# Feature projection in fp32 by Strassen's seven block products, with GpSimd making the weight sums

## What is computed

```python
mod = jax.nn.silu(c) @ p['ada_w'] + p['ada_b']
shift, scale, gate = jnp.split(mod, 3, axis=-1)
h = rms_norm(x, p['norm_w']) * (1 + scale[:, None, :]) + shift[:, None, :]
z = h @ p['w_in']
z_a = centred_conv3(z[..., :A_CONV_COLS], p['conv_a'])
...
y = jnp.concatenate([y_a, y_b, y_c], axis=-1) @ p['w_out']
return x + gate[:, None, :] * y
```

## Time and profile before

| | |
|---|---|
| time, median of 3 runs | 5318.88 us (5315.06 to 5323.39) |
| span of the profiled execution | 5309.2 us |
| TensorE busy | 5077.2 us, 96% |
| VectorE, ScalarE, GpSimd busy | 2811.0, 2089.1, 513.2 us |
| granted TensorE clock, mean | 0.983 |

### The profile page before, as it was taken

The page is one execution under the profiler, slowest core; times in us unless marked ns, Lnnn a source line. Parts: engine busy times, 40 slices in busy tenths (PEclk is TensorE's granted clock), DMA queues, the critical chain, the costliest instruction groups (busy, mean ns, idle before and its releaser), DMA issues. The chain is left out here.

```text
span 5309.2 us, 97761 instructions
## 1 busy us (share of the span) xinstructions
PE 5077.2 (96%) x40460; PEld 2651.3 (50%) x40460; DVE 2811.0 (53%) x4438; ACT 2089.1 (39%) x3590; POOL 513.2 (10%) x950
## 2 busy tenths in 40 slices
PE   8999999989979999989989999999899799999899
PEld 3444444468754444444434444444778544444454
DVE  2222387746645565556522223876566455555565
ACT  1121455346545444421111214553556445445211
POOL 0000000033320000001100000000344100000011
PEclk9999999999989999999999999999999899999999
DMA  6311566466650222145343115664666502221353
GB/s 230 142 68 60 191 207 212 141 172 169 166 138 19 56 57 47 37 142 210 117 164 142 70 60 187 219 200 153 173 168 167 129 14 55 56 50 38 123 174 112
DMA packets 549653, 668.51 MB, mean 126 GB/s; under 512 B 200976, under 2 KB 427792, under 8 KB 539168
## 3 DMA queue, kind: packets, MB, share of 16 engines
q1 hardware_dynamic: 548624, 661.17, 40.0%
q10 hardware_dynamic: 592, 1.10, 0.1%
HBM read 395.01 MB, written 267.13 MB: 125 GB/s over the span
## 5 line engine op out<-in xcount | busy, mean ns | idle before, releaser
L517 PE MATMUL ps<-feat_hT,w_features 128*128 128x512 f32 x2240 | 972.5, 592 | 0.0
L517 PEld LDWEIGHTS ps<-feat_hT,w_features 128*128 128x128 f32 x2240 | 420.4, 190 | 505.9 <-issue 503.2
L1968 DVE TENSOR_REDUCE att_mx<-ps 128x1 f32<-128x1024 f32 x384 | 453.2, 1219 | 282.3 <-PE ps L1844 280.4
L2256 PE MATMUL ps<-w_out,fin_yT 128*128 128x512 f32 x1280 | 568.6, 598 | 1.3 <-ACT fin_yT L2118 1.3
L850 PE MATMUL ps<-w_tokens,prep_hT 128*128 128x512 f32 (+1 forms) x1248 | 534.6, 586 | 0.0
L1863 PEld LDWEIGHTS ps<-kc,att_pr 128*128 128x128 f32 x3264 | 351.5, 141 | 322.8 <-issue 275.8
L1932 ACT ACTIVATE att_PT<-ps 128x512 f32<-128x512 f32 x384 | 229.0, 596 | 632.3 <-PE ps L1863 629.2
L1863 PE MATMUL ps<-kc,att_pr 128*128 128x128 f32 x3264 | 457.2, 280 | 5.8 <-ACT att_PT L1932 2.7
L1923 ACT ACTIVATE att_pr<-ps,att_nb 128x1024 f32<-128x1024 f32 x384 | 424.2, 1109 | 68.3 <-DVE att_nb L1970 68.1
L1977 DVE COPY att_PT<-ps 128x512 f32<-128x512 f32 x384 | 263.9, 687 | 285.1 <-PE ps L1863 284.5
L850 PEld LDWEIGHTS ps<-w_tokens,prep_hT 128*128 128x128 f32 x1248 | 234.8, 190 | 288.9 <-issue 285.2
(11 more groups left out here) (271 smaller groups left out, 6998.2 us busy)
## 6 DMA issues: line engine op xcount, KB each, us to landing
s_sc<-prep_sc SPq DMA_DIRECT2D x20, 3072.0 KB, 9.2
scan_src<-s_sc SPq DMA_DIRECT2D x104, 384.0 KB, 4.9
s_qkt<-scan_qT SPq DMA_DIRECT2D x40, 576.0 KB
s_zf<-feat_co SPq DMA_DIRECT2D x88, 256.0 KB, 2.6
src<-s_sc SPq DMA_DIRECT2D x56, 384.0 KB, 4.9
s_ht<-feat_hT SPq DMA_DIRECT2D x10, 2048.0 KB, 7.9
s_zt<-st SPq DMA_DIRECT2D x80, 256.0 KB, 4.5
fin_z<-s_zt SPq DMA_DIRECT2D x30, 576.0 KB, 5.4
```

What stands on the lines that cost most here:

```text
L517: last = pe.matmul(b, wf[:, k, i * P:(i + 1) * P], hT[g % 2][:, k, :], start=(k == 0), stop=(k == KD - 1))
L1968: ch.link(v.tensor_reduce(mx[:, n % 2, half:half + 1], ps[:, 2 * half:2 * half + 2, :].rearrange("p b n -> p (b n)"), AX.X, ALU.max))
L2256: last = pe.matmul(b, yT[n % TPG][:, k, :], wo[:, k, G * c:G * (c + 1)], start=(k == 0), stop=(k == KD - 1))
```

## The change

The 14 blocks are taken as seven pairs. For a pair and a group, the weights are a 2 x 2 arrangement of halves (block of the pair by half of the 1,024 rows), and so are the tokens (half of the rows by half of the 512 tokens). Strassen's algorithm, in Winograd's form, makes the 2 x 2 product from seven products of halves in place of eight. A product is now four weight tiles with 256 tokens moving.

- TensorE, per pair: `p1, p6, p5, p7, p2, p3, p4`, into the banks A, B, C, D, A, C, D. `p2`, `p3` and `p4` add to what is in the bank; `p2` waits until ScalarE has copied `p1` out, `p3` and `p4` until VectorE has read `p5` and `p7`. The turns of the next group stand behind `p2` of pairs 3, 4 and 5, in banks 4 to 7.
- GpSimd, per pair: four sums of weights, 128x512 each (`weight_sums`), two pairs ahead, in two buffers.
- VectorE: four sums of tokens per group, 128x1024 each (`token_sums`), and five combinations per pair, 128x256 each, in place of half of ScalarE's copies.
- ScalarE: two copies of 128x256 per pair in place of two of 128x512; its squares for the next group now stand behind pairs 0 and 1, two each.
- The first product of a group waits for all eight pieces of `hT`.
- `ada_w` gets six buffers (in `hT[1]`, the token sums and `wt_a`). The gate product is made in two halves, one after group 0 and one after group 1; each is eight products to one PSUM row range.
- `wt` is split: `wt_a` (512 columns) is loaded after group 1, the other 992 columns into `wf_a` during the last group, once pair 3 is done with it. `token_projection` reads from both and waits for the second part at its second piece.
- On SP's queue the tokens of group 1 now stand ahead of `hT` of group 0, and only 2 MiB of `ada_g` ahead of them.

```diff
+                def weight_sums(n):
+                    g, i = divmod(n, NPAIR)
+                    S = Ss[n % 2]
...
+                    if n >= 2:
+                        p.wait_ge(products, made_by_pe(n - 2, p3))
+                    p.tensor_tensor(S[:, 0, :, :], block_(1, 0), block_(1, 1), ALU.add).then_inc(sums, 1)
+                    p.wait_ge(sums, 4 * n + 1)
+                    p.tensor_tensor(S[:, 1, :, :], S[:, 0, :, :], block_(0, 0), ALU.subtract).then_inc(sums, 1)
+                    p.tensor_tensor(S[:, 2, :, :], block_(0, 0), block_(1, 0), ALU.subtract).then_inc(sums, 1)
+                    p.wait_ge(sums, 4 * n + 2)
+                    p.tensor_tensor(S[:, 3, :, :], block_(0, 1), S[:, 1, :, :], ALU.subtract).then_inc(sums, 1)
...
+                for n in range(NG * NPAIR):
+                    g, i = divmod(n, NPAIR)
+                    for m in (2 * i, 2 * i + 1):
+                        if m < NCONV:
+                            edge(g, m)
+                    if n + 2 < NG * NPAIR:
+                        weight_sums(n + 2)
...
+                    if not last:
+                        v.wait_ge(products, made_by_pe(n, p6))
+                        v.wait_ge(copied, n + 1)
+                        v.tensor_tensor(U, bank(BANK_B), U, ALU.add).then_inc(combined, 1)
+                    for g_, m in before[0:1]:
+                        side_taps(g_, m)
+                    if not last:
+                        v.wait_ge(products, made_by_pe(n, p5))
+                        v.tensor_tensor(u5[:, :], bank(BANK_C), U, ALU.add).then_inc(combined, 1)
+                    for g_, m in before[1:2]:
+                        side_taps(g_, m)
+                    if not last:
+                        v.wait_ge(products, made_by_pe(n, p7))
+                        v.tensor_tensor(output(g, 2 * i + 1)[:, HN:G], bank(BANK_D), u5[:, :], ALU.add).then_inc(combined, 1)
...
+                def product(n, bank_, weights, moving, start, stop):
+                    for k in range(HK):
+                        last = pe.matmul(ps[:, bank_, 0:HN], weights[:, k, :], moving[:, k, :], start=start and k == 0, stop=stop and k == HK - 1, skip_group_check=True)
+                    last.then_inc(products, 1)
...
+                    product(n, BANK_A, block_(0, 0), quarter(0, 0), True, False)
+                    pe.wait_ge(sums, 4 * n + 2)
+                    product(n, BANK_B, S[:, 1, :, :], Ts[:, 1, :, :], True, True)
+                    product(n, BANK_C, S[:, 0, :, :], Ts[:, 0, :, :], True, False)
+                    pe.wait_ge(sums, 4 * n + 3)
+                    product(n, BANK_D, S[:, 2, :, :], Ts[:, 2, :, :], True, False)
+                    pe.wait_ge(copied, n + 1)
+                    product(n, BANK_A, block_(0, 1), quarter(1, 0), False, True)
+                    if g + 1 < NG:
+                        for k in TURNS.get(i, ()):
+                            turn(g + 1, k)
+                    pe.wait_ge(sums, 4 * n + 4)
+                    pe.wait_ge(combined, made_by_dve(n, v_u5))
+                    product(n, BANK_C, S[:, 3, :, :], quarter(1, 1), False, True)
+                    pe.wait_ge(combined, made_by_dve(n, v_22))
+                    product(n, BANK_D, block_(1, 1), Ts[:, 3, :, :], False, True)
+                    if i == NPAIR - 1 and g < 2:
...
+                            last = pe.matmul(ps[64 * c:64 * c + 2, BANK_G, :], sg[:, k, :], wt_a[:, k, :], start=(k == 0), stop=(k == KD - 1))
```

More of the change, by code:

```diff
@@ L209, in modulation_columns, with feature_projection, weights_of, h_bank @@
     v.tensor_tensor(shift, made[:, 0, :, :, :], column(C_ADAB), ALU.add).then_inc(summed, 1)
[L212 to L236, removed]
+def feature_projection(l, wf_a, wf_b, wt_a, wt_in, wtb_in, hT0, h0_in, go, g_sent, st, src0, xc0, cols, sg, nc, d, ps, kc, col, amod, eps, ident):
+    NS, NO, NA = 4, 4, 6
+    NPAIR, HN, HK = NFB // 2, G // 2, KD // 2
+    BANK_A, BANK_B, BANK_C, BANK_D, BANK_H, BANK_G = 0, 1, 2, 3, 4, 7
+    PER = 7
+    TURNS = {3: (0, 1, 2), 4: (3, 4, 5), 5: (6, 7)}
+    FREED = 3
+    KEPT = 2 * (FREED + 1)
+    parts = [(0, 2), (2, 4), (4, KEPT), (KEPT, NFB)]
     def width(g):
         return G + 1 if g == NG - 1 else G
+    def weights_of(m0, m1):
+        return wf_a[:, :, m0 * P:m1 * P] if m1 <= KEPT else wf_b[:, :, (m0 - KEPT) * P:(m1 - KEPT) * P]
+    def h_bank(g, k):
+        return k if g == 0 else BANK_H + k % 4
     with ExitStack() as ctx:
@@ L254, in feature_projection @@
         mrows = sb("mrows", [P, 2 * 512]) if l == 0 else None
[L256 to L260, removed]
+        ada = [t for r in (wt_a[:, :, :].rearrange("p k n -> p (k n)"), hT[1][:, :, :].rearrange("p k n -> p (k n)"),
+                           Ts[:, :, :, :].rearrange("p q k n -> p (q k n)")) for t in (r[:, 0:2 * D], r[:, 2 * D:4 * D])]
+        with stage(nc, "x_in zeroed square_sums roots normed turned_in modulated copied c11 combined products sums t_made edges centre tapped conv kept0 kept1 o0 o1 o2 o3 first0 first1 first2 first3 "
+                       "c_in consts_in bias_in setd silu part0 part1 part2 part3 part4 part5 used made rows_s turned amod_s ada_g_in gate_made gate_s gate_sent wf0 wf1 wf2 wf3 wf4") as (
+                block, x_in, zeroed, square_sums, roots, normed, turned_in, modulated, copied, c11, combined, products, sums, t_made, edges, centre, tapped, conv, kept0, kept1, o0, o1, o2, o3, first0, first1, first2, first3,
+                c_in, consts_in, bias_in, setd, silu, part0, part1, part2, part3, part4, part5, used, made, rows_s, turned, amod_s, ada_g_in, gate_made, gate_s, gate_sent, wf0, wf1, wf2, wf3, wf4):
             kept, o_sent = (kept0, kept1), (o0, o1, o2, o3)
@@ L392, in _ @@
                     a.activation(sg[:, :, :], ct[:, :, :], ACT.Silu).then_inc(silu, 1)
-                square(0)
+                for j in range(TPG):
+                    square(0, j)
                 if l == 0:
@@ L464, in _ @@
                     modulate(0, k)
[L465 to L479 removed]
+                token_sums(0, (0, 1, 2, 3))
@@ L481, in _, with turn @@
             @block.tensor
             def _(pe):
+                def turn(g, k):
+                    b = h_bank(g, k)
+                    if g:
+                        pe.wait_ge(modulated, KD * g + k - 3)
+                        if k == 3 and g in (2, 3):
+                            pe.wait_ge(gate_s, g - 1)
+                    if k == 0:
+                        pe.wait_ge(normed, TPG * (g + 1))
+                    for j in range(TPG):
+                        last = pe.transpose(ps[:, b, j * P:(j + 1) * P], x[:, j, k * P:(k + 1) * P], ident)
+                    last.then_inc(turned_in, 1)
@@ L849, in project @@
                     for k in range(KD):
-                        last = pe.matmul(ps[:, tiles.bank(pieces[n]), 0:c1 - c0], hT[j % NH][:, k, :], wt[:, k, c0:c1], start=(k == 0), stop=(k == KD - 1))
+                        last = pe.matmul(ps[:, tiles.bank(pieces[n]), 0:c1 - c0], hT[j % NH][:, k, :], w[:, k, :], start=(k == 0), stop=(k == KD - 1))
                     last.then_inc(z_filled, 1)
```

281 lines of the change are left out of this document (177 added, 104 removed).

## The result

The changed kernel takes **5235.3 us**, the median of four runs (5224.4 to 5241.8), against 5317.0 for the kernel before in four runs (5307.3 to 5323.4): ratio 0.984, 95% interval 0.982 to 0.987. The forecast was 5236.0, with a range from 5214 to 5276. The profiled execution took 5241.8 us, the longest of the four.

A forecast was written before the change was run, and what follows sets the result against it. TensorE, busy 5077 of 5309 us, was taken as the bound. 115 - 13.5 - 8 - 3.6 - 4 - 3.2 - 0.3 = 82.4 us saved gave a span of 5227 and a median of 5236.5; likeliest 5236, range 5214 to 5276.

The forecast's parts named there:

- Products: Feature products on TensorE: 56 records of 0.2158 us make a pair 12.09 us instead of 13.73; 70 pairs save 115 us.
- rival of records that don't cost half: Product records of 256 columns cost more than 0.216 us; from 0.237 the kernel is slower than before; chance 0.07.
- Gate halves: Gate product: each half stands alone at 6.9 us, two take 13.7 instead of 7.0; 13.5 us lost.
- The shared ports: VectorE's taps held by GpSimd's weight sums in pairs 0, 1, 2 and 6: 0.2 us in 40 pairs, 8 us lost.
- The rival's two figures: Port as bound: taps lose to sums every time; 66 us lost (5294) with 1.6 us sums, 24 (5252) with 1.33; chance 0.22.
- Layer 0's start: First product waits for all scalings and token sums: net 3.6 us lost, plus 4 for slow clock and late tokens.
- slow clock and late tokens: Layer 0's first pairs: TensorE's clock falls after a gap, group 1's tokens delay `u5`; they cover each other, 4 us lost.
- Layer 1's start: First product waits for the scalings and token sums, 3.2 us lost; group 1's tokens make `u5` 0.3 us late.
- Costed at nothing: Loads: group 2's tokens come sooner, and the late 992 columns do not delay the token stage; 0 us.

The follow-up runs named there:

- the later one: The changed kernel run again with nothing altered, against the kernel before (5319.6 us, nine runs): 5230.9 us, ratio 0.983.

## Why the prediction was right, and where its terms were off

The forecast met the median within a microsecond, better than its terms deserve. It had 82.4 us for the stages that the change touches; A and C gave 88.1, while the medians of this comparison differ by 81.7, 6.4 less; in the profiles what takes from the gain lies in stages that the change does not touch. That the two errors cancel is luck. The 9.7 us by which the median stood above the profiled span are also for the most part a difference between executions: in the runs on record the time is 1.8 us above the span of the same execution. The span was forecast at 5227; the two profiles of the changed kernel have 5240.0 and 5224.7.

- **Products**, 115 us: right. The record of 256 columns, worked out as 0.2158 us from 512 and 288 columns, is 0.216; the pair is 12.09. With an eighth product the gain is given back, 119.5 us for 70 of 1.73. The rival of records that don't cost half is out.
- **Gate halves**, 13.5: 6.96 each in place of 7.04 for both, 13.8 in all. Right, and shown by the half that takes 3.56 when its two parts run side by side.
- **The shared ports**, 8 us: the step that failed in size. Leaving the sums out wins nothing, so the term is 0. The prediction had the third combination end at 8.05 us of the pair without a hold and at 10.65 with every tap behind the sums, against 10.36 when it is wanted. It ends at 9.15. The sums take 1.27 us and not 1.33, and end at 6.5 and not at 7; the taps begin at 4.5 in the pair shown and not at 4.1, and only the last of the four sums meets them. So 1.1 us of the 2.3 to spare are used, and 1.2 remain. The rival's two figures, 24 and 66 us, took every tap to lose. In the pair shown that happens only with twice the sums.
- **Normalising beside the first sums** was missing: 3.0 us, in layer 1 alone. There the first weights land at 2650.85, 0.4 us after the normalising begins, and GpSimd's first sum starts at 2650.92; the expectation that they had long been there was wrong. The prediction weighed the ports for taps only. The four instructions go from 2.74 to 5.76 us beside the sums, and back to 2.74 when the sums wait. The Trainium skill, page "SBUF — State Buffer", section "Who interferes with whom", counts VectorE's `tensor_scalar` among what can take both ports, and the trace agrees.
- **Layer 0's start**, 3.6 + 4: the first product came at 45.35 (forecast 44.8), the clock was at 0.50 from 45 to 47 us, the tokens landed by 63.16 (64.4) and made `u5` 0.62 late (0.8). By A, with 57.4 for 35 pairs and 6.9 for the gate, the start cost 57.4 - 6.9 - 43.8 = 6.7. Read directly it is 3.3 for the later first product, 1.6 for pair 0 (13.65 us in place of 12.09), 0.9 for pair 1 and 0.8 for pair 1 of group 1, 6.6 in all; the slow clock was costed at 3.1 and took the 1.6. In the other profile of the same kernel the slow clock lasts longer, pair 0 takes 0.9 more and pair 1 gives 0.6 of it back, so slow clock and late tokens do cover each other. So do the start and the tokens: an earlier start alone wins nothing, with earlier tokens 3.7 us.
- **Layer 1's start**, 3.2 + 0.3: the waits were 2.12 and 0.55, with the clock at 1.00 under the products and no late tokens. By C: 57.4 - 6.9 - 44.3 - 3.0 = 3.2. Read directly, the first product came 2.5 us later behind the end of the normalising than before, and pair 0 took 0.9 more than 12.09.
- **Costed at nothing**: the late 992 columns are waited for nowhere; the token stages took 530.6 and 529.4 us against 529.3 and 529.6.

So 8 us of ports too much, 3 us of normalising too little and 0.9 us too much for the start of layer 0 make, but for some tenths, the 5.7 us between 82.4 and 88.1. The two starts by A and C are what the other terms leave, so that this sum has to close; the direct readings agree with them within 0.3 us. The medians of the first comparison differ by 81.7, those of the later one by 88.6.

## What to carry to other kernels

When work goes to a neighbour that shares ports, find the instruction whose lateness reaches the bound engine and count its room in one period; held instructions are free up to that point, and beyond it each period pays. Count also what else stands in the helper's list: with twice the sums its own small work came late, which cost 17 us beside some 24. Check the first period by itself: there the helper starts as soon as its data land, next to work that steady periods never meet, and a wait that cures one collision can make the next. And where a stage outside the change moves by more than the effect, compare the touched stages from first instruction to first instruction.

## What was not expected of the hardware

A hold may be paid twice: in layer 1 the granted clock was 0.50 behind a wait of 2.54 us before `p6`, and the next 24 records cost another 1.7 us. With twice the weight sums it was 0.50 behind a wait of 2.40 us before `p5` as well, in pair 3 of group 3 of both layers. But in the run of the earlier first products a wait of 2.44 us before `p2` left it at 1.00, so that the wait alone does not decide it, and what does is not shown. A scan stage with the same instructions took between 484.4 and 498.4 us, at a mean clock of 0.97 in both of these; what makes the difference was not found.
